# Row gathers over all 128 partitions, and a down-projection over both array halves, in a mixture-of-experts step

## The reference

```python
h = rmsnorm(x, norm1_g);  proj = h @ w_in                      # 1024 -> 1536
ya = chunk_spatial_gate(u, v, a_ws, a_bs, chunk_len)           # from gelu(proj), 4 heads
yb = multiscale_pool(p, pool_prefix, pos, b_w, b_scale)        # windows 2, 4, 8, 16
x = x + jnp.concatenate([ya, yb], axis=-1) @ w_out
h2 = rmsnorm(x, norm2_g)
eidx, gates = hier_route(h2, r1_w, r1_b, r2_w, r2_b)           # group of 4, then 2 of 8 experts
x = x + moe_ffn(h2, eidx, gates, exp_w1, exp_w3, exp_w2)
y = rmsnorm(x, normf_g)
```

## Time and profile before

| | us |
|---|---|
| median of 3 runs (1023.95 to 1026.57) | 1025.72 |
| the profiled execution | 1025.62 |
| its span | 1024.0 |
| PE busy | 921.0 (90%) |
| DVE busy | 247.6 (24%) |
| POOL busy | 157.4 (15%) |
| ACT busy | 111.0 (11%) |
| DMA, mean over the span | 252 GB/s |

### The profile page before, as it was taken

How to read it: one execution, slowest core, us unless ns; L and a number is a source line. 1 busy time by engine, 2 the same in 40 slices (tenths; PEclk the granted TensorE clock), 3 DMA queues, 4 the chain that set the end, 5 groups by cost and what they waited for, 6 DMA issues and landing times. The chain is left out here.

```text
span 1024.0 us, 24939 instructions
## 1 busy us (share of the span) xinstructions
PE 921.0 (90%) x10522; PEld 587.5 (57%) x10522; DVE 247.6 (24%) x760; ACT 111.0 (11%) x172; POOL 157.4 (15%) x239
## 2 busy tenths in 40 slices
PE   5999999999999973999999999989988999898940
PEld 2545545455455542876777677657556685674620
DVE  1434452454534553410000000000000000000006
ACT  0211110111101110001010101010010010010004
POOL 1000000000000002112222222212112122112110
PEclk9999999999999995999999999999989999998985
DMA  8760010100101063999999999999999999999938
GB/s 340 277 251 21 22 41 0 41 21 21 41 0 43 39 247 98 394 366 390 363 387 363 370 367 369 368 372 376 368 390 375 379 384 380 355 389 363 326 70 322
DMA packets 57935, 258.22 MB, mean 252 GB/s; under 512 B 11410, under 2 KB 12490, under 8 KB 40853
## 3 DMA queue, kind: packets, MB, share of 16 engines
q1 hardware_dynamic: 47740, 238.54, 60.6%
q0 software_dynamic: 10144, 18.95, 8.1%
HBM read 234.55 MB, written 24.60 MB: 253 GB/s over the span
## 5 line engine op out<-in xcount | busy, mean ns | idle before, releaser
L1186 PEld LDWEIGHTS ps<-hT,big 128*64 128x64 f32 x8192 | 286.4, 138 | 40.1 <-issue 28.6
L1186 PE MATMUL ps<-hT,big 128*64 128x64 f32 (+8 forms) x8192 | 294.7, 233 | 14.7 <-DMA big<-in_exp_w 7.9
L1202 PE MATMUL ps<-big,poolT 128*64 128x512 f32 (+8 forms) x512 | 233.8, 609 | 11.3 <-DMA big<-in_exp_w 7.5
L1083 PE MATMUL ps<-big,hT 128*128 128x512 f32 x384 | 169.9, 602 | 3.3 <-DMA big<-in_w_in 1.9
L1202 PEld LDWEIGHTS ps<-big,poolT 128*64 128x64 f32 (+8 forms) x512 | 75.1, 152 | 145.8 <-issue 135.2
L985 DVE TENSOR_TENSOR poolT<-u,ps 128x256 f32<-128x256 f32 (+8 forms) x32 | 15.1, 472 | 505.1 <-PE ps L1186 467.4
L1083 PEld LDWEIGHTS ps<-big,hT 128*128 128x128 f32 x384 | 73.2, 193 | 94.6 <-issue 88.5
L545 POOL DMA_INDIRECT x_rows<-xn,sidx x32 | 49.4, 1545 | 385.3 <-ACT xn L695 363.3
L695 ACT ACTIVATE xn<-ps,gslot 64x1024 f32<-64x1024 f32 (+8 forms) x32 | 35.5, 1110 | 456.0 <-PE ps L1202 240.8
L525 POOL DMA_INDIRECT slot_table<-ids,dest x18 | 18.7, 1038 | 328.2 <-DVE dest L807 271.9
L1140 PE MATMUL ps<-big,yT 128*128 128x512 f32 x128 | 56.4, 593 | 0.9 <-DVE yT L874 0.9
(11 more groups left out here) (168 smaller groups left out, 469.1 us busy)
## 6 DMA issues: line engine op xcount, KB each, us to landing
big<-in_exp_w SPq DMA_DIRECT2D x192, 1024.0 KB, 25.9
big<-in_w_in SPq DMA_DIRECT2D x4, 1536.0 KB, 13.5
big<-in_w_out SPq DMA_DIRECT2D x2, 2048.0 KB, 14.9
x_rows<-xres SPq DMA_DIRECT2D x8, 512.0 KB
h_rows<-xn SPq DMA_DIRECT2D x8, 512.0 KB, 2.7
big<-x_rows SPq DMA_DIRECT2D x8, 512.0 KB, 7.3
out_y_prompt<-big SPq DMA_DIRECT2D x8, 512.0 KB, 2.9
xres<-in_x_prompt SPq DMA_DIRECT2D x1, 3072.0 KB, 11.1
```

What stands on the lines that cost most here:

```text
L1083: last = pe.matmul(ps[0:m, bank, :], hT[:, k, 0:m], win[:, k, part * AW:(part + 1) * AW], start=(k == 0), stop=(k == KD - 1))
L1186: last = pe.matmul(out[c * w:(c + 1) * w, j, 0:m], up_weights(n)[:, k, j * P + c * w:j * P + (c + 1) * w], xT[:, 4 * half + k, 0:m], start ...
L1202: last = pe.matmul(ps[0:m, 5 + cols, :], hhT[:, 2 * half + k, 0:m], down_weights(n)[:, k, cols * 512:(cols + 1) * 512], start=(half + k == ...
```

## The change

1. **The table in SBUF.** A second copy, `spread`, is loaded by four transfers ahead of `tabs`. Slot w*32+i of an expert lies in partition w+4i. Gathers take their indices from it, over all 128 partitions, whatever the block's cap. The gate values and the scatters go on using `tabs`.
2. **The turn.** `turn_rows` replaces the eight transposes by eight matmuls of all 128 partitions of `xg` against `pick[:, 0:m]`, a permuted identity that puts the rows back into slot order. `pick` is made by DVE in the step of the second tile, in place of one block of `band_first`, which is no longer in use by then.
3. **The down-projection in halves.** For blocks of up to 64 rows (second blocks of pairs 1 to 9) the first 512 output columns go to partitions 0 to 63 of bank 5 and the other 512 to partitions 64 to 127 of bank 6, from the two column halves of the array. ACT evicts the first half, DVE the second with a product by the gate, and POOL's scatter waits for both.

```diff
-SMALL = max(c[1] for _, _, c in CLASSES)
+def in_halves(m):
+    return m <= NS
...
+        spread = sb("spread", [P, NE, 2], I32)
+        pick = band_first[:, 0, :]
...
             sp.wait_ge(table_stored, 16 * 2 * NT)
+            for w in range(WAYS):
+                sp.dma_start(spread[w:P:WAYS, :, :].rearrange("p e c -> p (e c)"),
+                             slot_table.rearrange("(r e) c -> r (e c)", e=NE)[w * P // WAYS:(w + 1) * P // WAYS, :])\
+                    .then_inc(spread_in, 16)
             sp.dma_start(tabs.rearrange("p e c -> p (e c)")[0:CAP, :],
...
-            def fetch(b, s, e, m):
-                pool.tensor_copy(gidx[s][0:m, :], entries(e, m, 0)).then_inc(gidx_ready, 1)
+            def fetch(b, s, e):
+                token = spread[:, e, 0:1] if isinstance(e, int) else spread[:, bass.ds(e, 1), 0]
+                pool.tensor_copy(gidx[s][:, :], token).then_inc(gidx_ready, 1)
...
-                gather(xg[s][0:m, :], gidx[s][0:m, :], rows_in[s])
+                gather(xg[s][:, :], gidx[s][:, :], rows_in[s])
...
                     pool.wait_ge(sidx_ready, count)
+                    if in_halves(m):
+                        pool.wait_ge(y_half_ready, h)
                     pool.wait_ge(y_ready, count)
...
-            pool.wait_ge(tabs_in, 16)
+            pool.wait_ge(spread_in, 16 * WAYS)
             for s in range(2):
-                fetch(s, s, FIRST + s, CAP)
+                fetch(s, s, FIRST + s)
+            pool.wait_ge(tabs_in, 16)
...
+                    if in_halves(m):
+                        act.activation(ys[s][0:m, 0:512], ps[0:m, 5, :], ACT.Copy,
+                                       scale=gslot[s][0:m, 0:1]).then_inc(y_ready, 1)
+                        continue
...
+                    dve.wait_ge(pooled, 1)
+                    dve.tensor_copy(pick.rearrange("p (w i) -> p w i", w=WAYS),
+                                    ident.rearrange("p (i w) -> p w i", w=WAYS)).then_inc(pick_made, 1)
...
                     if not (final and s):
                         take_xgT(b + 1, caps_of[1 - s])
+                    if in_halves(m):
+                        dve.wait_ge(rows_out[s], 16 * h)
+                        dve.wait_ge(gate_in[s], 16 * h + 16)
+                        dve.wait_ge(used, CH * b + CH)
+                        dve.tensor_tensor(ys[s][0:m, 512:D], ps[NS:NS + m, 6, :],
+                                          gslot[s][0:m, 0:1].to_broadcast([m, 512]), ALU.mult).then_inc(y_half_ready, 1)
...
+            def turn_rows(x, m, done):
+                xs = x[:, :].rearrange("t (p k) -> t k p", k=KD)
+                for c in range(KD):
+                    last = pe.matmul(ps[:, c // 4, (c % 4) * P:(c % 4) * P + m], xs[:, c, :], pick[:, 0:m],
+                                     start=True, stop=True, skip_group_check=True)
+                last.then_inc(done, 1)
...
-                        turn(xg[1 - s], max(caps_of[1 - s], SMALL), xgT_done)
+                        turn_rows(xg[1 - s], caps_of[1 - s], xgT_done)
...
                             for cols in range(2):
-                                last = pe.matmul(ps[0:m, 5 + cols, :], hhT[:, 2 * half + k, 0:m],
+                                first = NS * cols if in_halves(m) else 0
+                                last = pe.matmul(ps[first:first + m, 5 + cols, :], hhT[:, 2 * half + k, 0:m],
                                                  down_weights(n)[:, k, cols * 512:(cols + 1) * 512],
-                                                 start=(half + k == 0), stop=(half + k == 2))
+                                                 start=(half + k == 0), stop=(half + k == 2), skip_group_check=True)
...
-            turn(xg[0], CAP, xgT_done)
+            pe.wait_ge(pick_made, 1)
+            turn_rows(xg[0], CAP, xgT_done)
```

More of the change, by code:

```diff
@@ L36 @@
 SPLIT = 2
+WAYS = 4
 FIRST = NE - 2
 CLASSES = ((1, 4, (96, 56)), (4, 7, (88, 64)), (7, 10, (84, 64)), (10, 13, (80, 68)), (13, 16, (76, 72)))
-SMALL = max(c[1] for _, _, c in CLASSES)
 CH = 6
@@ L262, in build @@
         tabs_in = sem("tabs_in")
+        spread_in = sem("spread_in")
+        pick_made = sem("pick_made")
         chunk_in = [sem(f"chunk_in{c}") for c in range(2 * CH)]
@@ L275, in build @@
         y_ready = sem("y_ready")
+        y_half_ready = sem("y_half_ready")
         ov_free = sem("ov_free")
@@ L573, in block_pair @@
                         pool.wait_ge(rows_in[s], 16 * h + 16)
-                        fetch(b + 2, s, after[s], SMALL if s else m)
+                        fetch(b + 2, s, after[s])
                     if not_first(h):
@@ L587, in block_pair @@
                     pool.wait_ge(sidx_ready, count)
+                    if in_halves(m):
+                        pool.wait_ge(y_half_ready, h)
                     pool.wait_ge(y_ready, count)
                     scatter_add(ys[s][0:m, :], sidx[s][0:m, :], rows_out[s])
+            pool.wait_ge(spread_in, 16 * WAYS)
+            for s in range(2):
+                fetch(s, s, FIRST + s)
             pool.wait_ge(tabs_in, 16)
-            for s in range(2):
-                fetch(s, s, FIRST + s, CAP)
             pool.wait_ge(trash_zeroed, 16)
```

## The result

| | before | after |
|---|---|---|
| median, us | 1025.34 (1023.95 to 1026.57, 4 runs) | 1085.59 (1082.46 to 1093.74, 4 runs) |
| span of the profiled execution | 1024.0 | 1080.8 |
| PE busy | 921.0 (90%) | 1001.8 (93%) |

The change made the kernel slower: the ratio of the times is 1.0604, interval 1.0572 to 1.0636, some 60 us. The forecast was 999.

The account below looks back on a forecast made before the run. The prediction took the DMA engines' rate of moving weights as the bound: -33 us from the stream, +5 for coupling with PE and +1 at the start gave -27, so 1025.7 became 999 us, own range 987 to 1010, overall 987 to 1026.

Parts of the forecast that it names:

- The bound: Expert stage: the rate at which DMA engines move weight bytes limits the kernel, DMA share 1.01 over 571 us.
- Part 1: Gathers of 128 spread rows: weight loads no longer slowed beside 30 gathers, 33 us saved, at most 42.
- No change: Rival: reads of scattered rows cause the slowdown, so the stream stays at 370 GB/s; 1025 us, chance 0.14.
- Half of it: Rival: weight loads beside gathers stay slowed or partitions align only in part; 16 us saved, 1016 us, chance 0.17.
- 390 or more: Sign that the forecast is right: GB/s in the slices of the expert stage.
- the late landings of the earlier trace: Last gathers: 76 rows land in 13.4 to 18.9 us, 84 and 72 rows in 8.6 to 10.6; 2 us counted.
- SP's wait for PE: Weight loads: SP waits 80.6 us for PE to free chunks, but loads then queue 26 us (median).
- Part 2: Turn of gathered rows: 16 matmul instructions in 2.1 us, +1.0 per turn, +32 us of PE over 32 turns.
- Part 3: Down-projection in halves: 3.4 us less in each of nine blocks, 31 us less of PE.
- Part 4: Kernel start: four table loads at 0.35 us each delay the first gather; +1 us, bounds 0 and +3.
- Slower: Rival: the added turns decide as PE's pair passes the stream's; 1029 to 1033, say 1031 us, chance 0.10.
- PE's 34.6 us: Last six pairs: PE's work per pair, just under the stream's 35.1 us per 12 loads; coupling charged 5.

Follow-up runs that it names:

- e3: Kernel before with the change's gathers over 128 spread rows, turns still eight transposes with DVE restoring row order, down-projection whole: 1001.68 us, ratio 0.9778.
- e1: Kernel after, with the weights of a turn's matmuls taken from 128 neighbouring columns instead of every eighth: 1006.2 us, ratio 0.9803.
- e5: As e4, but slot r goes to partition r, so gathers name 128 partitions and rows are not spread: 1010.75 us, ratio 0.988.
- e4: e3 plus the down-projection in halves for blocks of up to 64 rows: 1002.71 us, ratio 0.9762.
- e11: e4 with scatters over 64, 80 or 96 partitions instead of 56 to 96, nothing skipped: 990.75 us, ratio 0.9686.
- e9: Kernel after, with the columns serving as a turn's weights 8 bytes apart instead of 32: 1005.06 us, ratio 0.9793.
- e10: Kernel after, with the columns serving as a turn's weights 16 bytes apart instead of 32: 1073.07 us, ratio 1.0455.
- e6: Kernel before with only the down-projection of its nine blocks of up to 64 rows in halves: 1024.2 us, ratio 1.0008.

## Why the prediction was wrong

**The bound and Part 1: right in the mechanism, too high in size.** The weight stream was the bound, and it was slowed by the company of the gathers. e3 has the clean gathers and PE's old work, and took 1001.68 us; e1, the change with its turn at the price that was forecast, took 1006.2 where 999 was forecast, inside the forecast's own range of 987 to 1010. 1.01 of DMA share became 1.00 at 385 GB/s instead of 370. The partitions were the cause (423 to 429 GB/s beside a gather, e3 and e5), not the reads of scattered rows, so *No change* fell, and *Half of it* too. The size was less than forecast: the stage gave back 22 us (571 to 549), not 33, and ran at 385 GB/s, where 390 or more was the sign. The prediction also took the late landings of the earlier trace rows for a trait of gathers of 76 rows. They were not: with 128 partitions the gathers of the end still took up to 16.8 us (e4), a median of 13.8, and it was e11, which changed only the scatters ahead of them, that brought them to 9.0. And SP's wait for PE was 151 us and not the 80.6 of one of its two rows; it didn't set the end, since a load then still stood 26 us in the queue.

**Part 2, the turn: the step that failed.** The forecast had 16 instructions at 0.131 us, 2.1 us in all and +1.0 per turn, with bounds of 0 and 32 us. Measured: 4.05 us, +2.9 per turn, 94 us over 32 turns, three times the upper bound. The price came from L1094: the right instruction, on weights that lie side by side. L1032, the transposes, read columns 32 bytes apart, but is one instruction per transpose and isn't slowed by it. Neither row had both, a matmul of this type and columns apart. I noted what the two rows had in common (128x128 weights) and not in what they differed from the new instruction, and so two equal numbers passed for two bounds. e1, e9 and e10 show that the distance alone makes the difference.

The Trainium skill speaks against this step (SBUF — State Buffer, "Door 1: The DMA port swizzle"): it says that reads within one 16-byte line go at full rate if two or more fall into it, and that each step to a new line costs. I had not weighed it. By it a turn at 32 bytes would be slow, without saying how much; the trace agrees at 8, 16 and 32 bytes (2.12, 3.96, 4.05 us). Its figure of four fp32 values as the free distance is not borne out: two are free, four are not. Nor does it tell why the transposes, at 32 bytes, are not slowed.

**From 94 us of turns to 60 of time.** One of the 32 turns lies ahead of the first up-projection. From the first up-projection to the last matmul the kernel before took 580.1 us (405.69 to 985.75), the kernel after 634.8 (409.58 to 1044.35). The terms: +91 for 31 turns; -31 for the halves, which now counted in full; -24, for PE's idle time in these stretches shrank from 28.8 us to 4.7; and the rest, some 19, is time at the lower clock. The granted clock is 0.98 over the stage before and 0.95 after, which is 0.02 x 571 = 11 us and 0.05 x 597 = 30 us, 19 more. It shows most plainly behind a turn. Timeline and windows of the kernel after:

```profile
466.23 4.06 PE L1201 MATMUL ps<-band_first,xg 128*128 128x56 f32 x16
470.09 8.73 PE L1242 MATMUL ps<-big,poolT 128*96 128x512 f32 x16
```

```profile
466.20:470.10 3.90, 3.90 (x21) 3.87 (x17) 0.56 (x1) 0.00 (x0) 0.00 (x0) 0.99 1.03 428
470.00:473.40 3.40, 3.40 (x6) 1.28 (x6) 0.62 (x1) 0.00 (x0) 0.00 (x0) 0.50 0.92 376
```

During the turn the clock is at 2.4 GHz, right behind it at 1.2 GHz, though PE had no idle time by its records; the down-projection took 8.73 us instead of 7.0. This followed 16 of the 31 turns and not the others: nine whole down-projections took 8.08 to 8.76 us instead of 7.04, seven halved ones 4.84 to 5.20 instead of 3.65, some 22 us in all. What sets these 16 apart was not found. That the slow turns bring this about is shown only in so far as e1, which has the same instructions with faster weight loads, has a granted clock of 1.00.

**Part 3: right in its size, wrong place.** 3.65 us instead of 7.04 at the full clock, as forecast. With the stream as the bound it brought nothing (e4 as fast as e3, e6 as fast as before), which the forecast had as well: its gain was to pay for the turns. It did pay, 31 us of 94.

**Part 4: +1 forecast, about +4 measured.** PE's first turn of the kernel before, then the start of the kernel after, of SP, POOL and PE:

```profile
403.09 1.54 PE L1032 MATMUL ps<-ident,xg 96*128 96x96 f32 x8 [9.34 <-DMA xg<-h_rows,gidx]
```

```profile
396.06 2.44 SPq L463 DMA_DIRECT2D spread<-slot_table  x4
...
401.04 1.09 POOL L549 DMA_INDIRECT xg<-h_rows,gidx  x1 [0.86 <-POOL gidx L575]
...
404.40 4.13 PE L1201 MATMUL ps<-band_first,xg 128*128 128x96 f32 x16 [10.73 <-DMA xg<-h_rows,gidx]
...
409.58 13.58 PE L1225 MATMUL ps<-hT,big 128*64 128x96 f32 x256 [1.05 <-DVE hT L1002]
```

Four strided loads cost 2.44 us, not 4 x 0.35, so the gather leaves 2.0 us later than in the earlier trace rows; the turn adds 2.6 (4.13 against 1.54), and the gather itself gives 0.7 back. Little of the 2.6 is the distance of the columns: this turn runs at a granted clock of 0.50, where the one of e1 takes 3.73 us.

**The rivals.** What happened is *Slower*, 0.10, by its mechanism: PE's pair passed the stream's. In a late pair PE is busy for 40.39 of 40.48 us (window 864.52 to 905.00 above), where the stream needs 35 by the forecast (36 by e3's stage, 549 us for 184 loads): two turns at +2.9 on the 32.56 of the earlier trace rows, and a clock of 0.96. But its price, 1031, used the same 2.1 us and so fell short as well. The sign to look for stood in the prediction ("PE busy without a break in pairs 10 to 15 with few loads outstanding"). The error was one of chance too: PE's 34.6 us stood against 35.1 of the stream, so every microsecond of error in the turn's price went on the path, and a step with a price taken from rows of other instructions deserved a wide range on its upper side.

## What to carry to other kernels

A price from a neighbouring row holds only if the row has the same instruction, the same size and the same layout of its operands; write down which of these differ before calling it a bound. Where a change hands a bound from one engine to another with half a microsecond to spare, give the terms of the second engine the range, not those of the first. Transfers that run beside a stream should name all 128 partitions (with skipped entries): here that took 13 us off, and 24 with the rows spread over them. A number that 16 divides does not do the same (beside the gather of 96 rows the stream ran at 306 GB/s), but for the scatters it took another 12 us off. A saving on the engine that waits took off nothing.

## What the runs showed of the hardware

- A float32 matmul's 128x128 weights load in 196 to 200 ns (a turn of 16, whose loads overlap, in 2.0 to 2.1 us) from columns 4 or 8 bytes apart and in 328 to 334 ns (4.0 us) from columns 16 or 32 bytes apart. At a granted clock of 0.50 the turn from neighbouring columns takes 3.73 us (e1) and the one from columns 32 bytes apart 4.13 (kernel after): the latter hardly depends on the clock. The transposes, which read the same rows 32 bytes apart, are not slowed: 1.16 us for eight. Why they escape was not settled.
- An indirect gather over 128 partitions leaves a stream of weight loads at 423 to 429 GB/s; one over 72 to 96 partitions pulls it to some 305.
- TensorE's granted clock can be 0.50 for 3.4 us without an idle moment of PE in the records, behind 4 us that the weight loads had filled (3.87 of 3.90 us). It followed 16 of 31 such turns.
- Not settled: whether there is a faster order with matmul turns and the columns laid side by side in memory; e1 suggests 1006 us, no better than the transposes' 1002.
